# Layer B's attention reordered: projection tiles in parts, two homes for queries and keys, output projection in two passes

## What is computed

```
q_dil, q_mem = split(rmsnorm(x) @ w_in)            # 12 dilated heads, 4 memory heads
k_sh, v_sh   = split(rmsnorm_kv(h) @ w_kv_shared)  # shared keys and values
for g, (window, dilation) in enumerate(((128,1),(512,4),(2048,16))):
    o_g, lse_g = dilated_window_attention(q[g], k[g], v[g])   # softmax with ALiBi
alpha = softmax(stack(lse), axis=0)                # the three groups share one denominator
o = concat(o_g * alpha[g], memory_attention(q_mem, mem))
x = x + o @ w_out
x = x + conv_ffn(rmsnorm(x))
```

## Time and profile before

| | us |
|---|---|
| median of 3 runs | 1313.81 (1313.54 to 1314.25) |
| the profiled execution | 1317.49, span 1315.7 |
| PE busy | 1236.4 (94%) |
| VectorE, ScalarE, GpSimd busy | 794.0, 555.4, 105.6 |
| mean granted PE clock | 0.976 of 2.4 GHz |

### The profile page before, as it was taken

The page is one execution under the profiler, slowest core; times in us unless marked ns, Lnnn a source line. Parts: engine busy times, 40 slices in busy tenths (PEclk is TensorE's granted clock), DMA queues, the critical chain, the costliest instruction groups (busy, mean ns, idle before and its releaser), DMA issues.

```text
span 1315.7 us, 16934 instructions
## 1 busy us (share of the span) xinstructions
PE 1236.4 (94%) x5975; PEld 1014.6 (77%) x5975; DVE 794.0 (60%) x1235; ACT 555.4 (42%) x918; POOL 105.6 (8%) x133
## 2 busy tenths in 40 slices
PE   5889999989999999999999897777999999999998
PEld 4767888768788888878887676666878888887886
DVE  4866666654777777732267566554477777775225
ACT  5536656644444444421254442423344444442223
POOL 0201333332000000000020000000300000000000
PEclk9989999999999999999999897898999999999999
DMA  7412121113333333323321221111333333332642
GB/s 227 129 32 64 50 65 49 49 41 89 97 96 96 96 96 96 97 95 97 127 64 52 61 67 47 49 49 33 97 88 100 98 97 96 96 96 82 161 123 83
DMA packets 183893, 112.50 MB, mean 86 GB/s; under 512 B 20063, under 2 KB 176031, under 8 KB 183839
## 3 DMA queue, kind: packets, MB, share of 16 engines
q1 hardware_dynamic: 183838, 111.79, 28.9%
HBM read 107.58 MB, written 2.10 MB: 83 GB/s over the span
## 4 chain that ended last, share of the span: by engine, by line
PE 83%; DVE 11%; ACT 3%; issue 2%; DMA 1%; POOL 0%; SPq 0%; DVEq 0%; ACTq 0%; POOLq 0%
PE bank L1281 17%; PE bank L1283 17%; PE bank L1282 17%; PE bank L1569 7%; PE bank L1542 7%; PE bank L1433 2%; PE bank L1434 2%; PE bank L1435 2%; DVE w_lo L848 2%; PE bank L1555 2%; PE bank L1491 2%; PE bank L1582 1%; PE bank L1691 1%; PE bank L1469 1%; PE bank L1509 1%
## 5 line engine op out<-in xcount | busy, mean ns | idle before, releaser
L1281 PE MATMUL bank<-y_hi,w_hi 128*128 128x512 f32 x928 | 367.6, 396 | 2.8 <-DVE w_lo L848 2.5
L1282 PE MATMUL bank<-y_lo,w_hi 128*128 128x512 f32 x928 | 363.2, 391 | 0.0
L1283 PE MATMUL bank<-y_hi,w_lo 128*128 128x512 f32 x928 | 363.1, 391 | 0.0
L556 ACT ACTIVATE w_hi<-raw 128x1024 fp32r<-128x1024 f32 x186 | 196.5, 1056 | 355.5 <-PE bank L1283 180.1
L848 DVE TENSOR_TENSOR w_lo<-raw,w_hi 128x1024 fp32r<-128x1024 f32 x188 | 229.9, 1223 | 160.3 <-ACT w_hi L556 157.7
L1281 PEld LDWEIGHTS bank<-y_hi,w_hi 128*128 128x128 f32 x928 | 175.5, 189 | 41.8 <-issue 4.7
L1282 PEld LDWEIGHTS bank<-y_lo,w_hi 128*128 128x128 f32 x928 | 175.5, 189 | 37.0 <-issue 1.2
L1283 PEld LDWEIGHTS bank<-y_hi,w_lo 128*128 128x128 f32 x928 | 175.3, 189 | 36.9
L1542 PE MATMUL bank<-ar,w_hi 128*128 (+1 forms) x288 | 88.8, 389 | 0.8 <-DVE af L1066 0.8
L715 ACT ACTIVATE af<-af,conv 128x512 f32<-128x512 f32 x88 | 63.0, 716 | 36.0 <-DVE af L1066 36.0
L1569 PE MATMUL bank<-w_hi,ar 128*128 128x512 f32 x288 | 77.1, 390 | 0.8 <-DVE af L1066 0.8
(11 more groups left out here) (189 smaller groups left out, 1638.1 us busy)
## 6 DMA issues: line engine op xcount, KB each, us to landing
raw<-in_a_ffn_up SPq DMA_DIRECT2D x44, 512.0 KB, 3.8
raw<-in_b_ffn_up SPq DMA_DIRECT2D x44, 512.0 KB, 3.8
raw<-in_a_ffn_down SPq DMA_DIRECT2D x22, 512.0 KB, 3.3
raw<-in_b_ffn_down SPq DMA_DIRECT2D x22, 512.0 KB, 3.7
raw<-in_a_w_in SPq DMA_DIRECT2D x20, 512.0 KB, 3.8
raw<-in_w_kv_shared SPq DMA_DIRECT2D x12, 512.0 KB, 3.9
raw<-in_a_w_out SPq DMA_DIRECT2D x8, 512.0 KB, 3.8
raw<-in_b_w_in SPq DMA_DIRECT2D x8, 512.0 KB, 3.9
```

Source lines behind the costliest of these rows:

```text
L556: nc.scalar.activation(w_hi[:, m % SPLIT, :], raw[:, m % RAW, :], ACT.Copy).then_inc(hi_done, 1)
L1281: mm(bank, w[0], y[0][:, k, :], start=(k == 0), stop=False)
L1282: mm(bank, w[0], y[1][:, k, :], start=False, stop=False)
L1283: last = mm(bank, w[1], y[0][:, k, :], start=False, stop=(k == KT - 1))
```

## The change

The order of layer B's attention is one new list, which takes in the memory slots (M). Projection tiles are listed in parts, P(jj,s,a,b) for k-steps a to b-1, and only the last part has the tile's event. Tile (4,2) moves behind (5,0) and (5,1), also in the order of loads. Queries and keys of pair 1 lie in the memory queries' region, those of pairs 3 and 5 in bm, with other waits ahead of their high parts. The scaling of the scores is taken apart into steps W(jp,b), one for each batch. The output projection goes in two passes over the 8 output tiles q: the first over k = 0, 2, 4, 6 (q 0 to 7), the second over 7, 1, 3, 5 (q 8 to 15); each pass is added to hT by itself. Its weights are loaded by halves of k and two output tiles at a time, 512 KB as before. Layer A's code is only renamed.

```diff
@@ -149,7 +149,8 @@
         qmB = ar[:, 0:2048].rearrange("p (s f t) -> p s f t", s=2, f=2)
         pmTB = ar[:, 4096:6144].rearrange("p (s k t) -> p s k t", s=2, k=2)
-        qkB = ar[:, 8192:10240].rearrange("p (x s t) -> p x s t", x=2, s=2)
+        qkB = [t.rearrange("p (x s t) -> p x s t", x=2, s=2) for t in
+               (ar[:, 8192:10240], ar[:, 0:2048], ar[:, 8192:10240], bm[:], ar[:, 8192:10240], bm[:])]
         pT = [(ar[:, 10240:10752], ar[:, 10752:11264]), (oT_hi[:, 5, :], oT_lo[:, 5, :])]
         vB = ar[:, 19456:22528].rearrange("p (g s k f) -> p g s k f", g=3, s=2, k=TT)
         act_hi = ar[:, 0:11264].rearrange("p (k t) -> p k t", k=FT)
...
@@ -302,28 +303,52 @@
-        SEQ_B = [("S", 0), ("P", 1, 0), ("P", 1, 1), ("P", 1, 2), ("V", 1), ("S", 1), ("P", 2, 0), ("P", 2, 1), ("P", 2, 2),
-                 ("V", 2), ("S", 2), ("P", 3, 0), ("G", 0), ("P", 3, 1), ("R", 0),
...
-                 ("P", 5, 0), ("T", 0, 6), ("T", 0, 7), ("A", 0, 6), ("P", 5, 1), ("A", 0, 7), ("P", 5, 2), ("V", 5), ("S", 5)]
...
-        for b in range(9):
-            SEQ_B += ([("T", 1, b)] if b < 8 else []) + ([("A", 1, b - 1)] if b else [])
-            if b in (0, 1, 2, 5, 6):
-                SEQ_B.append(left.pop(0))
-        OUT_B = [t[1:] for t in SEQ_B if t[0] == "O"]
+        B_TILES = [(0, 0), (0, 1), (0, 2), (1, 0), (1, 1), (1, 2), (2, 0), (2, 1), (2, 2), (3, 0), (3, 1), (3, 2),
+                   (4, 0), (4, 1), (5, 0), (5, 1), (4, 2), (5, 2)]
+        OUT_KS_B = [[0, 2, 4, 6], [7, 1, 3, 5]]
+        early = [("O", q, k) for q in range(KT) for k in OUT_KS_B[0]]
+        def outs(count):
+            return [early.pop(0) for _ in range(count)]
+        SEQ_B = [("P", 0, 0, 0, 5),
+                 ("M", 0), ("P", 0, 0, 5, 8), ("P", 0, 1, 0, 4),
+                 ("M", 1), ("P", 0, 1, 4, 8), ("P", 0, 2, 0, 3),
+                 ("M", 2), ("P", 0, 2, 3, 8), ("P", 1, 0, 0, 2),
+                 ("M", 3), ("V", 0), ("P", 1, 0, 2, 8), ("P", 1, 1, 0, 1),
+                 ("M", 4), ("P", 1, 1, 1, 8),
+                 ("M", 5), ("S", 0), ("P", 1, 2, 0, 8), ("P", 2, 0, 0, 4),
+                 ("S", 1), ("V", 1), ("P", 2, 0, 4, 8), ("P", 2, 1, 0, 8), ("P", 2, 2, 0, 5),
+                 ("S", 2), ("P", 2, 2, 5, 8), ("P", 3, 0, 0, 4), ("V", 2), ("P", 3, 0, 4, 8),
+                 ("G", 0), ("P", 3, 1, 0, 8), ("R", 0), ("W", 0, 0), ("W", 0, 1), ("P", 3, 2, 0, 3),
+                 ("T", 0, 0), ("T", 0, 1), ("W", 0, 2), ("W", 0, 3), ("P", 3, 2, 3, 6),
+                 ("A", 0, 0), ("T", 0, 2), ("P", 3, 2, 6, 8), ("A", 0, 1), ("T", 0, 3), ("P", 4, 0, 0, 3),
+                 ("A", 0, 2), ("P", 4, 0, 3, 5), ("A", 0, 3), ("W", 0, 4), ("W", 0, 5),
+                 ("S", 3), ("P", 4, 0, 5, 8), ("V", 3), ("P", 4, 1, 0, 5),
+                 ("T", 0, 4), ("T", 0, 5), ("W", 0, 6), ("W", 0, 7), ("P", 4, 1, 5, 8), ("P", 5, 0, 0, 1),
+                 ("A", 0, 4), ("T", 0, 6), ("P", 5, 0, 1, 4), ("A", 0, 5), ("T", 0, 7), ("P", 5, 0, 4, 8),
+                 ("A", 0, 6), ("S", 4), ("P", 5, 1, 0, 3), ("A", 0, 7), ("P", 5, 1, 3, 8), ("P", 4, 2, 0, 5),
+                 ("S", 5), ("P", 4, 2, 5, 8), ("P", 5, 2, 0, 3), ("V", 4), ("P", 5, 2, 3, 7),
+                 ("G", 1), ("P", 5, 2, 7, 8)] + outs(5) + [("R", 1), ("W", 1, 0), ("W", 1, 1)] + outs(3)
+        SEQ_B += [("T", 1, 0), ("T", 1, 1), ("W", 1, 2), ("W", 1, 3)] + outs(3)
+        for b in range(8):
+            SEQ_B += [("A", 1, b)] + ([("T", 1, b + 2)] if b < 6 else []) + ([("W", 1, b + 4)] if b < 4 else []) + \
+                ([("V", 5)] if b == 2 else []) + outs(3 if b < 7 else 0)
+        SEQ_B += [("O", q, k) for q in (KT, KT + 1) for k in (7, 1, 3)] + [("O", KT, 5), ("O", KT + 1, 5)]
+        SEQ_B += [("O", q, k) for q in range(KT + 2, 2 * KT) for k in OUT_KS_B[1]]
+        def nb(jj, s):
+            return N_ATB + B_TILES.index((jj, s))
...
@@ -405,10 +430,11 @@
             if n < N_ATB:
                 return cols(b_w_in[0], SBW + P * (n - N_QMB))
             if n < N_OUTB:
-                j, s = divmod(n - N_ATB, 3)
+                j, s = B_TILES[n - N_ATB]
                 j = B_ORDER[j]
                 return (cols(w_kv_shared, P * j), cols(b_w_in[0], P * j), cols(w_kv_shared, SBW + P * j))[s]
-            return cols(b_w_out[0], P * (n - N_OUTB))
+            u, e = divmod(n - N_OUTB, KT // 2)
+            return b_w_out[0].rearrange("(k u p) f -> u p k f", u=2, p=P)[u][:, :, 2 * P * e:2 * P * (e + 1)]
         block = ctx.enter_context(nc.Block())
...
@@ -766,24 +792,24 @@
                 ring(N_QMB + f + 2)
                 qk_high(14 + f, qmB[:, 0, f, :], 1)
-            def pair_event(jj, s):
-                n = N_ATB + 3 * jj + s
-                ring(n + 2)
+            def pair_event(jj, s, a, b):
+                if b < KT:
+                    return
+                ring(nb(jj, s) + 2)
                 if s < 2:
-                    if jj:
-                        act.wait_ge(sc_done, 2 * jj)
-                    qk_high(16 + 2 * jj + s, qkB[:, s, 0, :], 1)
+                    if jj == 1:
+                        act.wait_ge(ms_done, 2 * MH)
+                    elif jj == 3:
+                        act.wait_ge(mav, 2 * MH)
+                    elif jj:
+                        act.wait_ge(sc_done, {2: 2, 4: 6, 5: 8}[jj])
+                    qk_high(16 + 2 * jj + s, qkB[jj][:, s, 0, :], 1)
             def pair_v(jj):
                 if jj >= 3:
                     act.wait_ge(bav, (4, 6, 8)[jj - 3])
                 v_high(10 + jj, vB[:, jj % 3, 0, :, :], TR[:].rearrange("p (k f) -> p k f", k=TT))
-            for g in range(6):
-                mem_slot(1, g)
-                for n in finished(MEM_FILL_B[g], N_ATB):
-                    pair_event(0, n - N_ATB)
-            pair_v(0)
             def scores(jj):
...
@@ -813,12 +839,19 @@
                     act.wait_ge(bav, 8 * jp + b + 1)
                     nc.scalar.activation(hi, src, ACT.Copy).then_inc(o_hi, 1)
+            def out_event(q, k):
+                u, x = divmod(q, KT)
+                if k == OUT_KS_B[u][-1]:
+                    if x % 2:
+                        ring(N_OUTB + q // 2 + 2)
+                    if u:
+                        absorb(3, x)
             for op, *a in SEQ_B:
-                if op not in "OR":
-                    {"S": scores, "P": pair_event, "V": pair_v, "G": ratios, "T": batch_high, "A": output_high}[op](*a)
-            for k in range(KT):
-                ring(N_OUTB + k + 2)
-                absorb(3, k)
+                if op not in "RW":
+                    {"M": lambda g: mem_slot(1, g), "S": scores, "P": pair_event, "V": pair_v, "G": ratios,
+                     "T": batch_high, "A": output_high, "O": out_event}[op](*a)
             ffn(1, N_UPB, N_DNB)
             for t in range(TT):
...
@@ -1205,14 +1234,17 @@
                     ins = nc.vector.tensor_copy(coef0x[a, i], coef[a, 0])
                 ins.then_inc(co_spread, 1)
-            def scale_weights(jp):
+            def coefficients_natural(jp):
                 dve.wait_ge(co_back, jp + 1)
                 link(nc.vector.tensor_copy(coef0, TR[:, 32:40].rearrange("p (i h) -> p i h", i=4)))
-                for g in range(3):
-                    for hp in range(2):
-                        for i, (o, w) in enumerate(score_blocks(g, hp)):
-                            c = coef0[:, i, hp:hp + 1] if g == 0 else coef[:, g, hp, i:i + 1]
-                            nc.vector.tensor_scalar(scB[:, o:o + w], scB[:, o:o + w], c, None, ALU.mult).then_inc(scaled, 1)
+            def scale_weights(jp, b):
+                g, hp, blocks, _ = BATCHES[b]
+                for i in sorted(set(x[2] for x in blocks)):
+                    o, w = score_blocks(g, hp)[i]
+                    c = coef0[:, i, hp:hp + 1] if g == 0 else coef[:, g, hp, i:i + 1]
+                    nc.vector.tensor_scalar(scB[:, o:o + w], scB[:, o:o + w], c, None, ALU.mult).then_inc(scaled, 1)
             def batch_low(jp, b):
                 n = P * len(BATCHES[b][2])
...
@@ -1227,11 +1259,32 @@
                     dve.wait_ge(o_hi, PAIRS + hd + 1)
                     nc.vector.tensor_tensor(lo, src, hi.bitcast(F32), ALU.subtract).then_inc(o_ev, 1)
+            def out_event(q, k):
+                u, x = divmod(q, KT)
+                n = N_OUTB + q // 2
+                if k != OUT_KS_B[u][-1]:
+                    return
+                if x % 2:
+                    dve.wait_ge(tile_done, n + 1)
+                else:
+                    dve.wait_ge(o_mm, q // 2 + 1)
+                if u:
+                    dve.wait_ge(o_sum, q)
+                nc.vector.tensor_tensor(hT[:, x, :], hT[:, x, :], banks[x % 2][:], ALU.add).then_inc(o_sum, 1)
+                dve.wait_ge(o_sum, q + 1)
+                if u:
+                    nc.vector.engine_nop().then_inc(h_ready, 1)
+                if x % 2:
+                    nc.vector.engine_nop().then_inc(evicted, 1)
+                    ring(n + 2)
```

(71 more changed lines are left out.)

46 lines of the change are left out of this document (20 added, 26 removed).

## The result

| | median of runs, us | ratio to before (95%) | profiled span |
|---|---|---|---|
| before | 1313.67 | | 1315.7 |
| changed kernel | 1273.41 (1270.74 to 1274.66) | 0.9684 (0.9669 to 0.9699) | 1271.2 |

Faster by 40.3 us, where 39.8 was forecast. In the two profiles the same stretch, from tile (0,0) to the FFN's first matmul, went from 252.5 us to 207.6: 44.9 us. The profiled execution of before was 3.8 us above its median, that of after at its median, so the traces show more than the medians.

The account below looks back on a forecast made before the run. PE was held by latencies of chains through VectorE and ScalarE, and low clock. Floor 199.0 + pieces 1.0 + idle 10.7 + clock 2.0 = 212.7 us against 252.5, saving 39.8: 1313.8 - 39.8 = 1274.0 us, range 1262 to 1291.

Parts of the forecast that it names:

- memory heads: Memory heads' slots: 7 k-steps in each slot cover the waits of transposes and values; 0 to 0.2 us idle left.
- T(0,0): First transposes of the second softmax's weights: VectorE's chain outlasts the cover of 3 k-steps; 0.95 us idle left.
- A(0,5): Values step in the attention's first half: emptying of the output bank stands late in VectorE's queue; 1.9 us idle.
- Floor 199.0: Tile (0,0) to the FFN's first matmul: PE's same work at full clock without idle time, 199.0 us.
- pieces 1.0: Whole stretch: about 15 more switches from small matmuls to a 512-column step, 0.06 us each, 1.0 us.
- Clock 2.0: Clock staying low, mainly around the idle stretch in the first half's values steps: 2.0 us, between bounds 0 and 16.6.
- Sum 212.7: Tile (0,0) to the FFN's first matmul: work, pieces, idle time and low clock together, 212.7 us where 252.5 stood.
- Two homes: Queries and keys in two regions: tiles can be computed ahead of the previous pair's scores, no instruction added; cost 0.
- The second pass: Output projection's last 32 k-steps: VectorE needs 2.05 us per pass against PE's 2.73, so the additions to hT cost 0.
- Rival 1: Layer B's attention: VectorE's queue falls further behind, idle 22 us instead of 11; 1285 us, chance 0.13.
- Rivals 2 and 3: Layer B's attention: clock keeps dipping, 1288 us, chance 0.10; piecewise part held at 1.2 GHz, 1325 us, chance 0.05.
- Rival 4: Layer B's attention: waits move with the pieces, two thirds of idle time (24 of 37) return; 1298 us, chance 0.05.

Follow-up runs that it names:

- one-pass run: The changed kernel, but with the output projection in one pass over 8 k-steps per tile as before: 1278.9 us, ratio 0.9718.

## Why the prediction was right

Step by step against the changed kernel's trace:

| step | forecast, us idle | measured |
|---|---|---|
| memory heads | 0 | 0 |
| T(0,0) | 0.95 | 0.75 |
| tile (5,0) | 0.85 | 1.02 |
| A(0,4) | 1.25 | 0.82 |
| T(0,6) | 0.7 | 0.45 |
| A(0,5) | 1.9 | 1.68 |
| S(5) | 1.25 | 1.10 |
| V4 | 0.7 | 0.44 |
| q=1 | 1.5 | 1.39 |
| T(1,2) | 0.5 | 0.30 |
| A(1,7) | 0.65 | 0.74 |
| small ones | 0.4 | 0.5, in gaps too short to be listed |
| FFN's first tile | 0 | 0.38, and 0.45 inside it, behind the stretch |

- Floor 199.0 and pieces 1.0: PE was busy for 198.1. The two terms together were too high by 1.9 us. The clock in the rows is rounded to 0.01, which is up to 0.005 x 215.6 = 1.1 us of the floor; how the rest divides between floor and pieces is open.
- Clock 2.0: it cost nothing; the granted clock was 1.00 in each stage. It did not fall behind the wait of 1.68 us; in the runs above it fell in a wait of 7.2 us, behind 2.0 and 1.9 us in near succession, and behind 1.66 us in the second half of the one-pass run. So the bound that I drew from no single wait reaching 2 us would not have held there. The row that I took for the other bound, 34% idle at 1.00, has 0.74 in the row right behind it.
- Sum 212.7 against 207.6 measured: 5 us too long, of which 2 clock, 2 work, 1 waits. That the forecast of the median still hit to 0.6 us is luck in part, and the step that failed can be named: I said that the 3.7 us between profile and median of before lie outside of what changes. The stretch moved by 44.9 us in the profiles and the median by 40.3. Going by the one other profile that can be laid beside it, some 2.9 of the 3.7 us lay inside: in the run with the scalings split, the same steps with the same waits took 99.1 us from tile (0,0) to T(0,0), where the profile of before has 102.0. The runs without a trace agree, as their granted clock over the whole span is on record: the profiled execution had 0.976 at 1317.49 us; beside the split, ten runs of before had 0.979 or 0.980 at 1313.0 to 1316.3 us, and one had 0.976, at 1318.93. So the profile of before held more low clock than the median run, the saving of the median was put too high by some 3 to 4 us for that, and the sum that was 5 us too long made up for it.
- Two homes at cost 0: right, and their absence costs 10 us.
- The second pass at cost 0: wrong by 0.8 us. The FFN's wait on q=14's addition was said to lie 2.7 us in the past; the addition runs from 900.59 for 0.67 us, and the FFN's first matmul waits for it until 901.31. The prediction had named a wait on its own additions as a sign of being wrong; this sign came, at 0.38 us. The term was VectorE's 2.05 us per pass, from durations measured 5.5 us apart; at 2.7 us apart VectorE and GpSimd meet, two passes take it 6.1, and PE feels it after eight.
- Rival 1 (VectorE's queue) is out: idle time was 9.6 us and not 22, and 6.7 us more went by order alone. Rivals 2 and 3 (clock) are out by the rows at 1.00. Rival 4 is out by the same 9.6 us, where it had 24; its time was also mis-added, since 24 us of idle time in place of 10.7 give 1287 and not 1298.

The Trainium skill has the encounter of VectorE and GpSimd in "GPSIMD Engine Reference", section "8. Key points": GpSimd shares its SBUF interfaces with VectorE and contends with instructions there that read two SBUF inputs. This case agrees: w_lo and y_lo, with two such inputs, were slowed (to 1.52 and 1.77 us), the addition to hT with one input in PSUM was not (0.68).

## What to carry to other kernels

Where one engine has all the work and stands idle for chains through others, write down each queue's order with durations from the trace and look for the item that a deadline stands behind; filler of the length of the chain removes the wait and the low clock that follows it. Count what a missing wait would cost only once: one part's saving may be another's already. When steps are moved closer together, ask which engines now run at the same moment that took turns before.

## What the hardware showed that I had not expected

- VectorE and GpSimd, both on operations with two SBUF operands: in the pairs shown above, the one that started second took the delay. y_lo 0.74 became 1.77 behind GpSimd's 1.36; GpSimd's 1.36 became 1.74 behind y_lo's 0.74. One pair in the kernel before is less clear: y_lo took 1.18 us though GpSimd's copy, an operation with one input, began 0.02 us after it.

```profile
913.73 1.18 DVE L854 SCALAR_TENSOR_TENSOR y_lo<-hT,gains,y_hi 128x512 fp32r<-128x512 f32 x1
```
```profile
913.75 0.61 POOL L498 COPY ss<-sq 128x512 f32<-128x512 f32 x1 [229.21 <-ACT sq L566]
```

- The granted clock stayed at 1.00 through 22.9 us with 17% idle in waits of up to 1.7 us, and was 0.90 over 34.7 us with 19% idle in waits of up to 1.7 us. In the kernel before, 12.2 us with 34% idle kept 1.00, and the next 6.5 us had 0.74. And the same steps with the same waits had 0.95 in one profile and 0.98 in another. I had priced the clock by the idle share and the longest wait of a stage; by these rows neither is a price.
- Behind a full 4-byte matmul (the squares) two matmuls are held up: the first takes 0.80 us where others take 0.40, and the one after it starts 0.64 us later, where between the others it is 0.23.
